# Output projection of a hybrid attention layer: work prepared within attention, three fp32r products in an unrolled tile loop

## What is computed

```python
def merge(o_a, o_b, g_a, g_b, w_out):
    return jnp.concatenate([head_rmsnorm(o_a, g_a), head_rmsnorm(o_b, g_b)], axis=-1) @ w_out

sh1, sc1, g1, sh2, sc2, g2 = modulation(c, w_ada, b_ada)
y = mixer(modulate(x, norm_mix, sh1, sc1), ...)          # projections, attention, merge
x = x + g1 * y
x = x + g2 * hier_moe(modulate(x, norm_ffn, sh2, sc2), ...)   # top-1 of 4 groups, top-2 of its 8 experts
```

## Time and profile before

| what | value |
|---|---|
| median of 3 runs | 1324.05 us (1323.19 to 1329.44) |
| profiled execution | 1330.6 us, span 1328.8 us, granted clock 0.939 |
| PE busy | 1160.6 us (87%) |
| PE weight loads busy, beside the matmuls | 766.3 us (58%) |
| DVE busy | 519.8 us (39%) |
| ACT busy | 340.1 us (26%) |
| POOL busy | 295.2 us (22%) |
| moved by DMA | 219.35 MB, mean 165 GB/s |

### The profile page before, as it was taken

The page is one execution under the profiler, slowest core; times in us unless marked ns, Lnnn a source line. Parts: engine busy times, 40 slices in busy tenths (PEclk is TensorE's granted clock), DMA queues, the critical chain, the costliest instruction groups (busy, mean ns, idle before and its releaser), DMA issues. The chain is left out here.

```text
span 1328.8 us, 19895 instructions
## 1 busy us (share of the span) xinstructions
PE 1160.6 (87%) x7175; PEld 766.3 (58%) x7175; DVE 519.8 (39%) x1320; ACT 340.1 (26%) x854; POOL 295.2 (22%) x233
## 2 busy tenths in 40 slices
PE   3778999999999999999976999991499989989966
PEld 1436988888888888888765455541133333333322
DVE  2432244444444454544552266656121111111128
ACT  3432133333333333333343212210011111111112
POOL 2031212122211212030002356533312212212001
PEclk9678999999999999999997999995699989999988
DMA  9772111111010313030203111110999999998876
GB/s 370 295 283 69 49 41 56 35 44 48 28 45 18 107 33 92 1 108 1 72 12 139 38 58 48 63 40 17 415 422 420 413 410 362 402 417 346 321 260 206
DMA packets 53764, 219.35 MB, mean 165 GB/s; under 512 B 9937, under 2 KB 26713, under 8 KB 42785
## 3 DMA queue, kind: packets, MB, share of 16 engines
q1 hardware_dynamic: 37138, 118.05, 24.5%
q10 hardware_dynamic: 7632, 82.05, 15.0%
q0 software_dynamic: 8896, 17.93, 3.5%
HBM read 197.41 MB, written 30.04 MB: 171 GB/s over the span
## 5 line engine op out<-in xcount | busy, mean ns | idle before, releaser
L727 PE MATMUL att_piece_ps<-hT_hi,w_hi 128*128 128x384 f32 (+1 forms) x528 | 185.6, 352 | 2.2 <-PEq L163 0.9
L1636 PE MATMUL moe_gu_ps<-moe_a_gu_sb,moe_xT_sb 128*64 x416 | 184.4, 596 | 3.2 <-DVE moe_xT_sb L1794 2.0
L1639 PE MATMUL moe_gu_ps<-moe_b_gu_sb,moe_xT_sb 128*64 128x512 f32 x416 | 184.4, 596 | 0.0
L727 PE MATMUL att_piece_ps<-hT_hi,w_lo 128*128 128x384 f32 (+1 forms) x528 | 173.9, 329 | 0.0
L727 PE MATMUL att_piece_ps<-hT_lo,w_hi 128*128 128x384 f32 (+1 forms) x528 | 173.5, 329 | 0.0
L914 DVE COPY att_pT_sb<-att_pT_ps 128x512 f32<-128x512 f32 (+2 forms) x192 | 94.5, 520 | 135.0 <-PE att_pT_ps L788 134.4
L1201 PE MATMUL mix_y_ps<-mix_w_out_sb,mix_oT_sb 128*128 128x512 f32 (+1 forms) x288 | 130.4, 612 | 2.2 <-ACT mix_oT_sb L1269 2.2
L1636 PEld LDWEIGHTS moe_gu_ps<-moe_a_gu_sb,moe_xT_sb 128*64 128x64 f32 x416 | 57.0, 138 | 123.0 <-issue 123.0
L975 ACT ACTIVATE att_probs_sb<-att_probs_sb,att_nmax_sb 128x640 f32<-128x640 f32 (+5 forms) x144 | 101.2, 703 | 43.5 <-DVE att_nmax_sb L900 42.7
L900 DVE CUSTOM_DVE_ANT_0 att_probs_sb<-att_s_ps,att_bias_sb 128x640 f32<-128x640 f32 (+5 forms) x144 | 95.2, 661 | 27.1 <-PE att_s_ps L776 14.6
L727 PEld LDWEIGHTS att_piece_ps<-hT_hi,w_hi 128*128 128x128 f32 x528 | 100.0, 189 | 9.7 <-issue 5.2
(11 more groups left out here) (288 smaller groups left out, 1805.7 us busy)
## 6 DMA issues: line engine op xcount, KB each, us to landing
moe_b_gu_sb<-in_w_gu ACTq DMA_DIRECT2D x26, 2048.0 KB, 18.4
moe_b_dn_sb<-in_w_dn ACTq DMA_DIRECT2D x26, 1024.0 KB, 12.1
moe_a_gu_sb<-in_w_gu SPq DMA_DIRECT2D x10, 2048.0 KB, 13.1
keep_rows_all_sb<-in_w_ada SPq DMA_DIRECT2D x8, 2048.0 KB, 12.6
att_w_raw_sb<-in_w_qkv SPq DMA_DIRECT2D x21, 512.0 KB, 3.3
moe_a_dn_sb<-in_w_dn SPq DMA_DIRECT2D x10, 1024.0 KB, 20.4
in_w_ada_sb<-in_w_ada SPq DMA_DIRECT2D x4, 2048.0 KB, 10.6
in_x_sb<-in_x_prompt SPq DMA_DIRECT2D x8, 512.0 KB, 7.0
```

The lines of the kernel that those rows point to most:

```text
L727: ins = pe.matmul(bank[:, 0:hi - lo], w[:, kind, kc, :], x[:, kc, lo:hi], start=(m == 0), stop=(m == 3 * NC - 1))
L1636: pe.matmul(gu_ps[p % 2][LANE[0], :], xT[:, c, LANE[0]], a_gu[:, bass.ds(slot, 1), c, :].rearrange("p a n -> p (a n)"), start=(c == 0), st ...
L1639: ins = pe.matmul(gu_ps[p % 2][LANE[1], :], xT[:, c, LANE[1]], b_gu[p % 3][:, c, :], start=(c == 0), stop=(c == NC - 1))
```

## The change

**Memory.** One arena takes the place of the tensors that came and went: the split activations hT and the split weights of attention lie at fixed places in it, and over them, once they are dead, the two halves of w_out, the rows of gate1, shift2 and scale2, and in the last stage expert weights.

**In attention.** SP loads w_out in eight slices of 512 KB into columns of rows_all that only the last pair fills; POOL scales a slice by the head norm's weights and splits it into hi and lo (two slices in a pair); SP stores both to a DRAM tensor. After the last projection POOL issues two loads of 4 MB that bring the halves back into the arena. The modulation columns are transposed once on PE, stored to DRAM, and loaded as broadcast rows by SP. ACT squares each unit's heads with a sum (`head_squares`), POOL's `normalise` makes the power and multiplies the rows, two pairs behind; for the last pair tile by tile.

**In the output stage.** The loop is unrolled over nine tiles, x, h2 and the transposed rows have two buffers, and ACT and DVE make hi and lo of the transposed rows. The projection is 48 fp32r matmuls in two halves with another tile's routing between them. `pick` becomes `choose` and `enter`; tiles 7 and 8 are chosen as one group. For tile 8 the two adds are DVE's.

**In the experts' stage** the rows of the second gate are loaded from the stored columns in pieces of 512 bytes instead of 4 KB rows.

```diff
@@ attention, sync
+        def load_wo(c):
+            if c:
+                sp.wait_ge(wo_stored, 32 * c)
+            sp.dma_start(wo_raw, in_columns(a["w_out"][:, c, :])).then_inc(wo_ld, 16)
+
+        def store_wo(c):
+            sp.wait_ge(wo_split, c + 1)
+            sp.dma_start(in_columns(k["w_out"][0, c]), wo_hi).then_inc(wo_stored, 16)
+            sp.dma_start(in_columns(k["w_out"][1, c]), wo_raw).then_inc(wo_stored, 16)
...
+                if n < PAIRS:
+                    store_wo(2 * n)
+                    load_wo(2 * n + 1)
                 if n + 2 < ALL:
                     load_w(3 * (n + 2))
...
+        sp.wait_ge(piece_ready, PARTS * ALL)
+        sp.wait_ge(gates_stored, 16)
+        for sec in range(3):
+            for cond in range(2):
+                r = DEC if cond else P
+                sp.dma_start(k["gate_home"][sec][0:r, cond, :].rearrange("p (c n) -> p c n", c=NC),
+                             rep(k["gates"][sec, :, cond, :], 0, r)).then_inc(k["gates_ld"], 16)
@@ attention, gpsimd
+            pool.tensor_scalar(wo_raw, wo_raw, col, None, ALU.mult).then_inc(wo_upper, 1)
+            pool.wait_ge(wo_upper, 2 * c + 1)
+            pool.tensor_copy(wo_hi.bitcast(F32R), wo_raw).then_inc(wo_upper, 1)
+            pool.wait_ge(wo_upper, 2 * c + 2)
+            pool.tensor_tensor(wo_raw.bitcast(F32R), wo_raw, wo_hi, ALU.subtract).then_inc(wo_split, 1)
...
+            if n >= 2:
+                normalise(n - 2, 0, TILES)
+            if n <= PAIRS:
+                split_wo(2 * n - 2)
+                split_wo(2 * n - 1)
+        pool.wait_ge(piece_ready, PARTS * ALL)
+        pool.wait_ge(wo_stored, 32 * NC)
+        for part in range(2):
+            pool.dma_start(k["w_out_home"][part][:, :, :], k["w_out"][part].rearrange("c p n -> p c n")).then_inc(k["w_out_ld"], 16)
+        normalise(ALL - 2, 0, TILES)
+        for t in range(TILES):
+            normalise(ALL - 1, t, t + 1)
@@ attention, scalar
+            for h in range(2):
+                ins = act.activation(squares[0:r, h, :], rows_all[0:r, t, first + HD * h:first + HD * h + HD], ACT.Square,
+                                     accum_out=head_ms[0:r, n % 2, 2 * at + h:2 * at + h + 1])
+            ins.then_inc(head_sums, 1)
...
+                if last:
+                    head_squares(*last)
                 columns_out(n, at)
@@ mix_out, tensor
+            for c in range(NC):
+                for part, w in ((oT_hi, w_hi), (oT_hi, w_lo), (oT_lo, w_hi)):
+                    ins = pe.matmul(y_ps[0:r, cols], part[j][:, c, 0:r], w[:, c, cols], start=(m == 0), stop=(m == 3 * NC - 1))
+                    m += 1
...
+        transpose_o(0)
+        pe.wait_ge(k["w_out_ld"], 32)
...
+        for t in range(TILES):
+            if t + 1 < TILES:
+                transpose_o(t + 1)
+            project(t, 0)
+            if t >= 2:
+                route(t - 2)
+            project(t, 1)
+            if t:
+                transpose_h(t - 1)
+            if ends(t - 2):
+                positions(t - 2)
+        route(NT - 1)
+        transpose_h(NT)
+        route(NT)
+        positions(NT)
@@ mix_out, vector
+        for t in range(TILES):
+            if t + 1 < TILES:
+                lower(t + 1)
+            if ends(t - 2):
+                choose(t - 2)
+            gated(t)
+            if ends(t - 2):
+                enter(t - 2)
+            mean_square(t)
+            scale_h2(t)
+        choose(NT)
+        enter(NT)
```

More of the change, by code:

```diff
@@ L502, in _, with pair_columns @@
                           rep(vecs[:, V_BADA + 8 * G1:V_BADA + 8 * (G2 + 1)], 2, 2), ALU.add).then_inc(mod_out, 1)
+def pair_columns(n):
+    first = n % PAIRS * P + (512 if banded(n) else 0)
+    return slice(first, first + P)
 def unit_keys(band, t):
@@ L543, in attention @@
     own_r = s.sb("own_r", [P, 4, P], F32R)
+    squares = s.sb("squares", [P, 2, HD])
+    head_ms, half = s.sb("head_ms", [P, 2, UNITS]), s.sb("minus_half", [P, UNITS])
+    wo_raw, wo_hi = (rows_all[:, 0:NT, pair_columns(n)] for n in (ALL - 1, ALL - 2))
+    gate_rows = rows_all[0:GATE_ROWS, NT, pair_columns(ALL - 1)]
     s_ps = [s.ps(f"s{j}", [P, 1024]) for j in range(2)]
@@ L987, in rows_out @@
             act.wait_ge(rden_done, u + 1)
-            first = n % PAIRS * P + (512 if banded(n) else 0)
+            first = pair_columns(n).start
+            if u == TILES * (ALL - 2):
+                act.wait_ge(wo_stored, 32 * NC)
+                act.wait_ge(gates_stored, 16)
             for h in range(2):
@@ L1168, in _ @@
+        for t in GROUPS[-1]:
+            scatter(t)
+        pool.wait_ge(listed, 32 * TILES)
         pool.wait_ge(x_zeroed, 3)
@@ new lines, in positions @@
+            pe.wait_ge(picked_done, n + 1)
+            if g[0]:
+                pe.wait_ge(slots_done, g[0])
+            for j, u in enumerate(g):
+                r = rows_of(u)
+                out = pos_ps[0:r, NE * j:NE * j + NE]
+                pe.matmul(out, earlier[0:r, 0:r], picked[0:r, j, :], start=True, stop=False)
+                for i in range(j):
+                    pe.matmul(out, ones[:, 0:r], picked[:, i, :], start=False, stop=False)
+                ins = pe.matmul(out, ones[:, 0:r], before[:, :], start=False, stop=True)
@@ new lines, in positions @@
+            if g[-1] == NT:
+                total = pos_ps[:, 2 * NE:3 * NE]
+                for j, u in enumerate(g):
+                    r = rows_of(u)
+                    pe.matmul(total, ones[0:r, :], picked[0:r, j, :], start=(j == 0), stop=False)
+                ins = pe.matmul(total, ones, before[:, :], start=False, stop=True)
+            ins.then_inc(pos_ready, 1)
+        transpose_o(0)
+        pe.wait_ge(k["w_out_ld"], 32)
+        pe.wait_ge(ld, 48)
+        pe.wait_ge(zeroed, 3)
@@ L1288, in _ @@
+        upper(0)
+        for t in range(TILES):
+            if t + 1 < TILES:
+                upper(t + 1)
+            if ends(t - 2):
+                exps(t - 2)
+            if t:
+                columns(t - 1)
+            square(t)
+        columns(NT)
+        exps(NT)
     @block.vector
     def _(dve):
-        dve.scalar_tensor_tensor(a2col[:, :, :], mod[:, SC2, :, :], 1.0, rep(vecs[:, V_NFFN:V_NFFN + 8], 2, 2),
-                                 ALU.add, ALU.mult).then_inc(gate_cols, 1)
@@ L1303, in gated, with lower @@
+        def lower(t):
+            r, j = rows_of(t), t % 2
+            dve.wait_ge(oT_upper, t + 1)
+            dve.tensor_tensor(oT_lo[j][:, :, 0:r], oT_ps[:, :, 0:r], oT_hi[j][:, :, 0:r], ALU.subtract).then_inc(oT_out, 1)
         def gated(t):
@@ new lines, in _ @@
+        for j in range(2):
+            own(dve.tensor_scalar(tok[:, j, :, :], consts[:, K_TOK:K_TOK + 4].rearrange("p (a b) -> p a b", a=2),
+                                  float(P * j), None, ALU.add))
+        lower(0)
+        dve.wait_ge(zeroed, 3)
+        dve.wait_ge(k["gates_ld"], 96)
+        dve.wait_ge(ld, 48)
+        for t in range(TILES):
+            if t + 1 < TILES:
+                lower(t + 1)
+            if ends(t - 2):
+                choose(t - 2)
+            gated(t)
+            if ends(t - 2):
+                enter(t - 2)
+            mean_square(t)
+            scale_h2(t)
```

557 lines of the change are left out of this document (280 added, 277 removed).

## The result

The changed kernel takes 1272.29 us (median of 4 runs, 1271.66 to 1275.98), against 1325.83 us of the kernel before in the runs beside it: ratio 0.960, 95% interval 0.957 to 0.963, 53.5 us less. The forecast was 1270, 54.3 less, in a range of 1254 to 1297. Two later sets of runs gave 1272.61 and 1274.64 us for the same kernel.

A forecast was written before the change was run, and what follows sets the result against it. PE bounds attention, weights the experts; the gain lies in the output stage's head and PE's work per tile. -22.9 - 29.4 - 6 + 4 = -54.3: 1330.6 becomes 1276.3, against the median about 1270 us; range 1254 to 1297.

The forecast's parts named there:

- A: Output stage's head, before the first projection: falls from 28.8 to 5.9 us with rows already normalised, -22.9 us.
- B: Output stage's nine tiles: 48 single fp32r passes at 0.234 us each, full period 15.9 us, -29.4 us.
- The cover on DVE and POOL: In the tiles, the DVE and POOL chain takes 13.7 us, so PE sets the period with 2 us to spare.
- C: Tail from the last projection to the table: 33.9 us becomes 27.8 with tiles 7 and 8 chosen together, -6 us.
- D: Attention: added weight splits, head norm and transfers are hidden except at the end, +4 us (bounds 2 and 36).
- The return: After the last attention projection, two 4 MB loads of the split weight take 25 to 47 us, hidden.
- Rival 1: In the tiles, DVE and POOL hold each other up and set the period: 1282 us, or 1288; chance 0.24.
- Rival 2: Attention pays 0.15 to 0.5 us per unit for squares ahead of ACT's copy: about 1290 us; chance 0.13.
- Rivals 3 and 4: Split weight returns late before the first projection, 1387 us, chance 0.04; 512-column matmuls run at 0.43 us, 1355 us, chance 0.02.
- Rival 5: More comes back: nothing paid in attention, no clock loss, a tail of 24 us: 1258 us; chance 0.06.
- Experts: Experts' stage: bound by weights as before, the second gate's rows arrive long before they are wanted, 0 us.

The follow-up runs named there:

- e2: Changed kernel with the output projection as 16 fp32 matmuls a tile, weight unrounded, in place of 48 fp32r ones: 1297.06 us.
- e3: Changed kernel with the projection's third product (low half of rows by high half of weight) left out, 32 matmuls a tile: 1254.65 us.
- e6: Changed kernel with tiles 7 and 8 chosen and entered one after the other instead of as one group: 1270.14 us.
- e5: Changed kernel without the head norm in attention (ACT's squares and POOL's normalise left out): 1277.22 us.
- e1: Changed kernel with each second pair of w_out stores, and the slice load behind it, put behind the next pair's cache loads in SP's queue: 1270.36 us.
- e4: Changed kernel with POOL's two 4 MB loads of the split weight issued at attention's very end, behind the last head norm: 1297.34 us.

## Why the prediction was right, and where its parts were not

**The profiled execution and the median.** The sum was made against 1330.6 and the difference carried over. The traces differ by 58.9 us, the medians by 53.5, as the profiled execution of before was some 5 us longer than its median. The four terms, forecast as -54.3, measure -57.7 (-22.1, -36.7, -6.2 and +7.3): the tiles gave 7.3 us more, attention took 3.3 more and the head gave 0.8 less. That the forecast lies within 1 us of the medians' difference is therefore partly luck: errors that cancel, and a long profile to start from.

**A, head, -22.9: right,** -22.1. The loads were called hidden with 4.9 us. They were not quite: PE reaches its wait for the mask, ahead of the second transposes, at 704.5 and stands there until 707.7, 0.8 us past the low half. The prediction had nearly right when the loads land (the mask 5.1 us after the stage's start); it did not look at what stands behind PE's wait for them.

**B, tiles, -29.4: mechanism right, size off,** -36.7. The 0.234 us for 512 columns, worked out from 384 and 320, is measured at 0.23. *e2* puts the form's share at 23.2 us, and 9 tiles x 2.5 would be 22.5. The missed 7.3 us are three small errors. Transposes, routing and positions were taken up to the ends of their groups, 4.7 us with 0.3 for the ends of products, and cost 3.8 by their starts, since each group starts before the one ahead has ended; the products took 11.4 and not 11.2, so a tile has 15.17 and not 15.9 us. PE waited 0.7 us in all where 2 were allowed. And the lower clock cost about 1.6 us, not 3, as it lasted for 8 matmuls of 0.43 instead of 0.23.

**The cover on DVE and POOL: right.** 13.7 us were worked out for the chain and 2 us of slack; *e3* shows 13.2 and 1.9. The chain was taken too long mainly in choose: between 913.87 and 917.76 stand 17 operations and not 15, 0.23 us each, and choose takes 4.3 us in a middle tile (774.71 to 778.98) instead of 4.9.

**C, tail, -6: right,** -6.2. But "about level with it", of the four scatters, was wrong by 1.2 us, and the order that brings them together is no gain (*e6*).

**D, attention, +4: too small,** +7.3. The end was right (+2.7). For the squares 1 us was taken in the last pair, and *e5* shows nothing even there. What failed is the sentence on SP's queue: behind each store "stands the load of the weights two pairs on: due a pair later, so hidden". Behind the second store of a pair stand also the value store and the cache load of the next pair, which PE wants within 9 us. *e1* shows it as some 3.2 us, about half of it the wait and half the lower clock behind it.

**The return: right.** 25 to 47 us were taken, 31 measured, and hidden; *e4* makes the cover visible. **Rival 1** has half of its hold in the trace: 2.26 us for L1516 in enter, and none in choose, where L1479, in the place of the L1348 of before, takes 0.16. It has no price: the step from the hold to a longer period did not follow, as DVE's 1.44 us ahead of gated were left. By the Trainium skill ("SBUF — State Buffer", "Who interferes with whom") a DVE operation with two inputs in SBUF contends with a GpSimd operation that reads SBUF; the row of L1516, with two tensors of SBUF, agrees. The prediction's own row for this, L1348, had one tensor and one value per row as its inputs; it too ended with a POOL operation, L1157. **Rival 2** falls with *e5*. **Rivals 3 and 4** fall with the trace: the weight had landed 12.7 us ahead of the stage, and 512 columns took 0.23 us. **Rival 5** falls with attention's +7.3. **Experts:** 0 taken; the measured difference is within what repeats show.

## What to carry to other kernels

Work moved under a stage bound by another engine was nearly free here while that engine waited on nobody; what it cost sat at the stage's last unit and in the transfer queue. So for each moved transfer list what stands behind it and when that is wanted, and count with a wait of TensorE that its clock can fall behind it. For a train of matmuls on PE, add the distances between starts and not the durations. When a tile loop is at the limit of one engine, cut one of its operations for a measurement: the new period is the length of the next chain, if the trace shows that engine waiting for it.

## What the runs showed that was not expected

Issuing transfers cost SP more behind the two w_out stores, which go in pieces of 512 bytes: 2.54 and 1.41 us for the two store issues behind those at 440, against 0.43 and 0.59 us in the kernel before. Whether the pieces or the number of transfers under way is the cause was not tested. A block that had issued software-queue loads at its end did not end until they had landed (*e4*: 24 us). Whether the router's input changes the experts' time by 6 us (*e5*) for the same number of matmuls was not followed up.
